# A diffusion layer with experts on one core: the first part of the modulation in four column stages, and tiles 0 and 1 projected together chunk by chunk

## What is computed

```python
m = silu(c) @ w_mod + b_mod                      # (6*D,), for c_ctx (prompt) and for c (latent): 2 conditions
sh1, sc1, g1, sh2, sc2, g2 = split(m, 6)
p = (rms_norm(x, norm1) * (1 + sc1) + sh1) @ w_in      # D=1024 -> 1536 = fourier 256 | q 768 | k 256 | v 256
u, q, k, v = split(p)
mix = concat(dft2(u) @ w_fourier, attention(q, k, v, sink))     # latent q, k rotated (rope)
x = x + g1 * (mix @ w_out)
x = x + g2 * moe(rms_norm(x, norm2) * (1 + sc2) + sh2)          # 64 experts, top 8, plus a shared one
return rms_norm(x, norm_f), k, v (of the prompt)
```

## Time and profile before

| | |
|---|---|
| median of 3 runs | 1045.42 us (1043.95 to 1045.7) |
| profiled execution, its own time | 1045.96 us |
| span of its trace | 1044.1 us |
| TensorE busy | 1005.5 us, 96% of the span |
| VectorE, ScalarE, GpSimd busy | 333.2, 227.0 and 161.5 us |
| chain that ended last | PE 80%, DMA 11%, DVE 5%, ACT 2% |
| mean granted TensorE clock | 0.993 |

### The profile page before, as it was taken

The page is one execution under the profiler, slowest core; times in us unless marked ns, Lnnn a source line. Parts: engine busy times, 40 slices in busy tenths (PEclk is TensorE's granted clock), DMA queues, the critical chain, the costliest instruction groups (busy, mean ns, idle before and its releaser), DMA issues.

```text
span 1044.1 us, 17787 instructions
## 1 busy us (share of the span) xinstructions
PE 1005.5 (96%) x7124; PEld 454.2 (44%) x7124; DVE 333.2 (32%) x839; ACT 227.0 (22%) x537; POOL 161.5 (15%) x233
## 2 busy tenths in 40 slices
PE   6999999999999999999999999999999999989996
PEld 3655556565455553444333333343333333423342
DVE  0122225865126772322111111121111111212388
ACT  1211104666122340112111111121111111212111
POOL 1000010300132022111221112112221121111000
PEclk9999999999999999999999999999999999989998
DMA  9965407500101199999999999999999999997896
GB/s 375 405 252 192 161 32 192 231 2 2 60 21 41 48 381 393 388 410 423 421 420 419 419 420 417 413 420 414 416 412 413 410 402 390 422 370 301 347 409 258
DMA packets 59676, 321.64 MB, mean 308 GB/s; under 512 B 9748, under 2 KB 10396, under 8 KB 31560
## 3 DMA queue, kind: packets, MB, share of 16 engines
q1 hardware_dynamic: 43184, 272.71, 65.0%
q0 software_dynamic: 14240, 43.34, 10.6%
q10 hardware_dynamic: 2168, 4.43, 1.1%
HBM read 298.78 MB, written 31.39 MB: 316 GB/s over the span
## 4 chain that ended last, share of the span: by engine, by line
PE 80%; DMA 11%; DVE 5%; ACT 2%; issue 1%; SPq 1%; POOLq 0%; DVEq 0%; ACTq 0%
PE bank L2120 27%; PE bank L2140 13%; PE bank L1711 8%; DMA ring<-in_w_up 7%; PE bank L1882 7%; PE bank L2092 4%; PE bank L1976 3%; PE bank L1738 2%; PE bank L1909 2%; PE bank L1700 2%; PE bank L1989 2%; DMA ring<-expert_rows 2%; PE bank L1895 2%; PE bank L1982 1%; PE bank L1866 1%
## 5 line engine op out<-in xcount | busy, mean ns | idle before, releaser
L2120 PE MATMUL bank<-ring,reg_h 128*32 128x512 f32 x2448 | 334.2, 595 | 6.3 <-DMA ring<-in_w_up 4.6
L2120 PEld LDWEIGHTS bank<-ring,reg_h 128*32 128x32 f32 x2448 | 99.3, 110 | 190.8 <-issue 190.7
L2140 PE MATMUL bank<-ring,reg_y 128*32 128x512 f32 x1224 | 170.5, 594 | 2.8 <-ACT reg_y L1075 2.0
L2120 PE MATMUL bank<-reg_p,reg_h 128*32 128x512 f32 x688 | 143.8, 602 | 0.5 <-DMA ring<-in_w_up 0.5
L1538 DVE TENSOR_TENSOR reg_h<-reg_p,bank 128x256 f32<-128x256 f32 x49 | 20.6, 421 | 320.8 <-ACT reg_p L1093 280.0
L1093 ACT ACTIVATE reg_p<-bank 128x256 f32<-128x256 f32 x49 | 18.8, 383 | 310.8 <-PE bank L2120 310.8
L1711 PE MATMUL bank<-ring,reg_h 128*128 128x384 f32 (+2 forms) x256 | 84.3, 487 | 0.0
L769 POOL DMA_INDIRECT expert_rows<-reg_y,rowc x47 | 47.2, 1004 | 239.6 <-DVE reg_y L1523 229.3
L2140 PEld LDWEIGHTS bank<-ring,reg_y 128*32 128x32 f32 x1224 | 46.5, 110 | 83.7 <-issue 79.1
L1523 DVE TENSOR_SCALAR reg_y<-bank,reg_p 128x512 f32<-128x512 f32 x49 | 36.8, 750 | 129.4 <-PE bank L2140 129.2
L2140 PE MATMUL bank<-reg_p,reg_y 128*32 128x512 f32 x344 | 72.3, 593 | 0.0
(11 more groups left out here) (279 smaller groups left out, 968.4 us busy)
## 6 DMA issues: line engine op xcount, KB each, us to landing
ring<-in_w_gate SPq DMA_DIRECT2D x51, 1024.0 KB, 13.7
ring<-in_w_up SPq DMA_DIRECT2D x51, 1024.0 KB, 22.2
ring<-in_w_down SPq DMA_DIRECT2D x51, 1024.0 KB, 20.3
ring<-in_w_mod SPq DMA_DIRECT2D x21, 1024.0 KB, 7.3
ring<-expert_rows SPq DMA_DIRECT2D x19, 1024.0 KB, 14.5
reg_p<-in_w_gate SPq DMA_DIRECT2D x13, 1024.0 KB, 12.8
reg_p<-in_w_up SPq DMA_DIRECT2D x13, 1024.0 KB, 20.5
reg_p<-in_w_down SPq DMA_DIRECT2D x13, 1024.0 KB, 23.7
```

What stands on the lines that cost most here:

```text
L2120: last = pe.matmul(bank[2 + p][R * j:R * j + R, :], xg_t[:, p, k * P + R * j:k * P + R * j + R], w_gu(homes[n % SLOTS])[:, k], start=(k == ...
L2140: last = pe.matmul(bank[y_banks(b)[hf]][R * j:R * j + R, :], h_t[:, p, i * P + R * j:i * P + R * j + R], w_dn(homes[n % SLOTS])[:, i, 512 ...
```

## The change

The modulation's first part is loaded in four stages of columns. Stage n holds, for all eight `k`, 256 columns of the shift and 256 of the scale (2 MB in two DMAs), which is what the chunks 2n and 2n+1 of both tiles need. Its products (`first_mod`) put the eight `k` into four bands, two after one another in each, so the bank holds partial sums; `first_columns` adds the bands with a small matmul, which also turns the rows into columns, and adds `b_mod` by a second one. `w_in`'s quarters are loaded behind the stages. `first_product(k, t)` multiplies chunk k for tile t, three matmuls of 512 columns, into banks 2 to 4 for tile 0 and 5 to 7 for tile 1. `mod_bias`, `first_projection` and the filler between the pieces are gone; later pieces 0 to 5 stand behind the two tiles.

```diff
             for n in range(4):
+                for part in range(2):
+                    o = D * part + 2 * P * n
+                    sp.dma_start(early_mod[n][:, part], wmod_v[:, :, o:o + 2 * P]).then_inc(s_piece[2 * n + part], 16)
+                if n == 0:
+                    sp.dma_start(xs[:, 1, :], x_sample[0, 0:P]).then_inc(s_x, 16)
                 sp.dma_start(view(ring, slot(n // 2) + 2 * PROJ * (n % 2), 2, PROJ), win_v[:, 2 * n:2 * n + 2, :])\
                   .then_inc(s_win[n], 16)
...
             for i in range(LATER):
-                sp.wait_ge(s_mpe, i + 1 if i < 4 else KD + i - 3)
+                sp.wait_ge(s_mpe, (1, 1, 1, 2)[i] if i < 4 else i + 1)
...
+            def h1_pair(n):
+                act.wait_ge(s_tr, n + 1)
+                act.wait_ge(s_a1, n + 1)
+                for t in range(2):
+                    for i in range(2):
+                        k = 2 * n + i
+                        last = act.activation(h1t[:, k, t * P:(t + 1) * P], bank[1][:, (2 * t + i) * P:(2 * t + i + 1) * P],
+                                              ACT.Identity, scale=a1[:, k, t:t + 1], bias=sh1[:, k, t:t + 1])
+                last.then_inc(s_h1k, 1)
...
+            for n in range(4):
+                h1_pair(n)
+            act.wait_ge(s_xl, 16)
+            squares(2, T, 3)
+            first_out(0)
...
+            def first_rows(n):
+                dve.wait_ge(s_mpe, n + 1)
+                dve.tensor_copy(mod_rows[0], bank[0][:, :]).then_inc(s_mrow, 1)
...
+            for t in range(2):
+                dve.wait_ge(s_std, t + 1)
+                link(dve.reciprocal(rstd[:, t:t + 1], rstd[:, t:t + 1]))
+                xhat(t)
+            for n in range(4):
+                first_rows(n)
+                first_columns(n)
...
+            def first_product(k, t):
+                w = view(ring, slot(k // 4), 4, PROJ)[:, k % 4, :]
+                for g in range(3):
+                    last = pe.matmul(bank[2 + 3 * t + g][:, :], h1t[:, k, t * P:(t + 1) * P], w[:, 512 * g:512 * g + 512],
+                                     start=(k == 0), stop=(k == KD - 1))
...
+            def first_mod(n):
+                for part in range(2):
+                    pe.wait_ge(s_piece[2 * n + part], 16)
+                at_least(pe, s_a1, n)
+                for k in range(KD):
+                    r = R * (k % 4)
+                    last = pe.matmul(bank[0][r:r + R, :], silu_w[:, k, :], early_mod[n][:, :, k, :], start=(k < 4), stop=(k >= 4))
+                last.then_inc(s_mpe, 1)
+
+            def first_columns(n):
+                pe.wait_ge(s_mrow, n + 1)
                 for j in range(4):
+                    row = KD * (j // 2) + 2 * n + j % 2
+                    pe.matmul(bank[0][:, 2 * j:2 * j + 2], mod_rows[0][:, j * P:(j + 1) * P], keep[:, C_SUM:C_SUM + 2],
+                              start=True, stop=False)
+                    last = pe.matmul(bank[0][:, 2 * j:2 * j + 2], b_rows, ident[0:2 * KD, row:row + 1].to_broadcast([2 * KD, 2]),
+                                     start=False, stop=True)
+                last.then_inc(s_mrt, 1)
+
+            def first_xhat_t(n):
+                if n:
+                    pe.wait_ge(s_h1k, n)
+                else:
+                    pe.wait_ge(s_xh, 2)
+                    pe.wait_ge(s_n1, 1)
...
+            busy(12)
             pe.wait_ge(s_silu, 1)
+            first_mod(0)
+            first_xhat_t(0)
+            first_columns(0)
+            busy(12)
+            for n in range(4):
+                pe.wait_ge(s_h1k, n + 1)
+                pe.wait_ge(s_win[n], 16)
+                if n < 3:
+                    first_product(2 * n, 0)
+                    first_product(2 * n, 1)
+                    first_mod(n + 1)
+                    first_xhat_t(n + 1)
+                    first_product(2 * n + 1, 0)
+                    first_columns(n + 1)
+                    first_product(2 * n + 1, 1)
+                else:
+                    first_product(2 * n, 0)
+                    first_product(2 * n + 1, 0)
+                    first_product(2 * n, 1)
+                    xhat_t(2)
+                    first_product(2 * n + 1, 1)
+            later_pieces(0)
+            later_pieces(1)
+            qk_t(0)
+            later_pieces(2)
```

More of the change, by code:

```diff
@@ L107, in shape_constants @@
     keep[:, C_COL + 4] = a + NQ
+    for cond in range(2):
+        keep[cond::R, C_SUM + cond] = 1.0
     tiles = np.zeros((E, 4, NQ), np.float32)
@@ L909, in _ @@
                 act.wait_ge(s_pa, 2 * t + 2)
[L910 to L917, removed]
+                act.copy(u_sb[:, t, :], bank[4][:, 0:FD]).then_inc(s_ea, 1)
+                q_out(t - 1)
             def fourier_y(n):
@@ L1176, in rows @@
             def rows(q):
[L1178 to L1186, removed]
+                dve.wait_ge(s_mpe, 4 + KD * q)
@@ new lines, in _ @@
+            dve.tensor_copy(upper[:], early[:, D_U:D_U + P]).then_inc(s_silu, 1)
+            by_unit = sink_in[:].rearrange("p (a b g) -> p a g b", a=2, b=2, g=3)
+            for a in range(2):
+                units = slice(6 * a, 6 * a + 6)
+                dve.tensor_copy(psink[:, units].rearrange("p (g b) -> p g b", g=3), by_unit[:, a])
+                dve.tensor_scalar(nsink[:, units].rearrange("p (g b) -> p g b", g=3), by_unit[:, a], -1.0, None, ALU.mult)
+            qk_out(0)
+            rotated(1)
@@ L1228, in _ @@
+            xhat(T - 1)
+            for t in range(2, T):
                 if t + 1 < T:
                     h1_half(t + 1)
-                if t and t + 3 < T:
-                    xhat(t + 3)
                 dve.wait_ge(s_pb, 2 * t + 1)
@@ L1784, in _ @@
-            last.then_inc(s_mrt, 1)
-            busy(6)
-            for t in range(T):
-                if t == 0:
-                    first_projection()
-                else:
-                    if t + 1 < T:
-                        xhat_t(t + 1)
-                    projection(t, (0, 1))
-                    if t == 1:
-                        later_pieces(0)
-                    later_pieces(2 * t - 1)
-                    if t == T - 1:
-                        channel_tables()
-                    projection(t, (2, 3))
-                    qk_t(t - 1)
-                if 0 < t < T - 1:
+            first_mod(0)
@@ L1801, in _ @@
+            later_pieces(0)
+            later_pieces(1)
+            qk_t(0)
+            later_pieces(2)
+            for t in range(2, T):
+                if t + 1 < T:
+                    xhat_t(t + 1)
+                projection(t, (0, 1))
+                later_pieces(2 * t - 1)
+                if t == T - 1:
+                    channel_tables()
+                projection(t, (2, 3))
+                qk_t(t - 1)
+                if t < T - 1:
                     later_pieces(2 * t)
-            pe.wait_ge(s_mrow, 3)
+            pe.wait_ge(s_mrow, 6)
```

225 lines of the change are left out of this document (102 added, 123 removed).

## The result

The changed kernel took **1056.30 us** (median of 4 runs, 1054.07 to 1058.29), the kernel before 1045.56 us beside it: a ratio of 1.0106, 95% interval 1.0088 to 1.0123. It is slower by 1.1% (10.7 us by the medians), where 0.1% (1.0 us) was forecast, and the time lies outside the range. A second run of the same kernel on another chip gave 1.0134 (1.0108 to 1.0161).

A forecast was written before the change was run, and what follows sets the result against it. TensorE's chain was taken as the bound. Start 11.1 us earlier and 1.7 us of wait gone, against three times 1.73 columns and 1.85 modulation, 1.3 transposes, 3.1 new wait: 1.0 us slower, 1046.4 us; range 1043.2 to 1050.0.

The forecast's parts named there:

- From there to the marker: From first product to start of tile 3's transposes: tiles 0 and 1 end at 76.1 us, that start at 85.5.
- When the first product can start: Kernel's start: loads, first modulation, columns and filler let the first product begin at 21.9 us, 11.1 us earlier than before.
- forecast marker: Start of tile 3's transposes on TensorE, forecast at 85.5 us against 84.5 before, 1.0 us slower.
- transposes of three stages: Stages 1 to 3: four transposes each at 0.44 us, 1.3 us in the sum.
- 96 product instructions: Tiles 0 and 1: 48 products of 512 columns at 0.86 us each, 41.3 us.
- end of the tiles to the marker: Behind tiles 0 and 1: later pieces 4 and 5 wait for their loads; tile 3's transposes start 9.4 us later.
- Loads: Start: w_mod's 1 KB rows load at 346 GB/s; stage 0's modulation lands at 12.6 us, tile 1's rows at 13.8.
- a low clock here as a rival: Start: TensorE still at 1.2 GHz, first product at 23.2 to 24.1 us, total up to 1048.7 us; chance 0.18.
- Columns: Small matmuls of first_columns: 16 instructions priced like the router's product, 0.108 us each, 1.73 us a stage.
- My faster rival: first_columns: stationary loads pass beside the products, 0.055 us an instruction or less; 2.4 us faster, 1043.0 us; chance 0.13.
- One to one behind the marker: From tile 3's transposes to the kernel's end: a shift of TensorE at 84.5 us passes on in full.
- The sum: Whole kernel: earlier start and removed wait against added columns, modulation, transposes and new wait; 1.0 us slower, median 1046.4 us.

The follow-up runs named there:

- filler_start: Changed kernel with 28 instead of 12 filler matmuls at the start and 6 behind the first modulation product; ratio 1.0097 against the kernel before.
- parts 3 and 4: Kernel before plus four extra blocks of small matmuls, four variants, ratios 1.0094 to 1.0153; then changed kernel with the bias through a 128-row stationary tile, 1.0046.
- cols_128rows: Changed kernel with the bias streamed through the identity, a 128-row stationary tile, instead of a 16-row one; ratio 1.0046 against the kernel before.
- later_apart: Changed kernel with later pieces 4 and 5 moved behind the first half of tile 2's projection; ratio 1.0080 against the kernel before.

## Why the prediction was wrong, point by point

The sign of the sum was right, the size not: 1.0 us was forecast, 10.7 measured. The step that failed is "**From there to the marker**", 7.1 of the 10.3 us: in it the 48 products at 0.86 us each, 41.3 us, which took 45.4, and the columns at 1.73 us a stage, which took 2.29. I priced the blocks by their own time, and that too low, and took everything behind them at the high clock. The other 3.2 us lie in "**When the first product can start**", in part for the same reason. Of the 10.3 us between the forecast marker (85.5) and the measured one (95.81), by the rows above:

| term of the sum | forecast | measured | difference |
|---|---|---|---|
| first product | 21.9 | 25.07 | 3.2 |
| three blocks of columns | 5.2 | 6.9 | 1.7 |
| transposes of three stages | 1.3 | 1.8 | 0.5 |
| 96 product instructions | 41.3 | 45.4 | 4.1 |
| end of the tiles to the marker | 9.4 | 10.2 | 0.8 |

- **Loads.** Right in rate: 346 GB/s was taken for 1 KB rows and 349 measured, so the rule of the Trainium skill that I had weighed (DMA: Bandwidth & Descriptors, Specifications: full rate from 512 B on) does not hold for these rows here. Stage 0's modulation had landed at 13.44 us instead of 12.6, and tile 1's rows were read at 14.73 instead of 13.8.
- **Start.** The form was right: `first_xhat_t(0)` began at 17.25 us, when `xhat(1)` was done (at the low clock `first_mod(0)` ended in the same moment, 17.21), and the filler, not ACT, set the start. Of the 3.2 us, 0.9 are the later landing. The four transposes took 1.11 us at the low clock, the block 2.5, nearly all of it at the high clock, and the filler 4.21 instead of 3.1, behind a new fall. I had a low clock here as a rival with 0.18 and 23.2 to 24.1 us, but one that stays low until the work has raised it; that the clock would come up and fall again behind the block was not in it. `filler_start` shows 1.65 us as the clock's.
- **Columns.** The term was mis-sized, 2.3 us for 1.73, because the row I took had no 16-row tile in it (parts 3 and 4). Four transposes took 0.59 us, and I had taken half of the eight of `L1726`, 0.44. My faster rival, which made them cheaper, had it the wrong way round.
- **Clock behind the blocks.** Missing from the prediction altogether. I had looked at the clock only at the start and only for pauses. It is 3.8 of the 4.1 us: with the clock up, the same instructions took 41.5 us in `cols_128rows`. Of the 3.8, 3.5 are the two falls and 0.3 the first product, which still began at the low clock.
- **Later pieces.** Right: the landing of piece 5 was forecast 8.4 us after piece 0 began and came 8.3 us after (85.58 to 93.84). Only the low clock on piece 5 (1.93 us for 0.93) was missing; of the six profiled executions with this wait it came in two, both of the changed kernel itself. `later_apart` shows that the wait was real.
- **One to one behind the marker.** Right as far as the attention (12.0 us there, of which 11.3 at the marker and 0.7 on tile 3's transposes), but at the end of the span only 8.2 in this pair of executions. Behind the attention the distance even grew, to 14.9 us at 904.55 us of the kernel before. Then it shrank to 11.6 us at the start of a row of 64 instructions and to 8.7 at its end: the kernel before had stood still for 4.03 us and then run at the low clock there, near 931 us, and took 9.98 us for them, the changed one stood still for 0.73 us and took 7.07 at 943.33 us. Why the distance grew and shrank is not shown. Single times of one kernel differ by 6 us, so one pair of profiles doesn't give this term.
- **The list under "The sum"** adds up to 2.3 us and not to 1.0: it leaves out the eight transposes of tile 1, which stood between the chunks before (0.87 us), and 0.4 us on tile 2's transposes and tile 1's products. The forecast itself, 76.1 + 9.4, has them.
- **The range** ended at 1050.0 us, since I added only one rival at a time to a sum in which three costs of the same sign were open.

## What to carry to other kernels

Matmuls that stream next to nothing are not cheap: with a new 128-column stationary tile each they took 0.105 us an instruction here, in turn with a tile of 16 rows 0.155, and behind most blocks of them that lasted 2.3 us and more the clock fell, which cost the dense work some 1.7 us each time. Transposes and a reduction on an idle VectorE avoided both (0.44 us a stage, no fall); pairs between long matmuls avoided only the fall. When work is pulled together, ask of each load what it waited behind before: here the loads of two pieces had been hidden by half a projection. And look at the granted clock in windows of the stretch that you change, not only at the mean of the span (0.986 here, 0.993 before). Compare equal instructions as well: in the kernel before the granted clock reads 1.00 up to 100 us, though twelve filler instructions took 2.86 us at 15.91 us and 1.54 at 20.10.

## What I had not expected of the hardware

- The clock fell while TensorE was busy without a gap (4.00 of 4.00 us at 0.61). It did so behind 15 of 20 blocks of 2.3 to 2.6 us between dense work, behind none of 11 of 1.7 us there, but behind one of 1.9 us at the start. It is not the same each time: 2 of 3 in one execution of the kernel and 3 of 3 in another, 1.7 us a block that come or don't.
- The number of rows of every second stationary tile (16 or 128) changed the time of a block from 1.68 to 2.29 us. Two instructions with 16-row tiles and two with 128-row tiles both took 0.31 us in turn, so the turn is dear and not one of the two; a block of 16-row tiles alone was not run.
- 64 streamed columns cost hardly more than 2 (1.73 against 1.68 us for 16 instructions).
